# Moving the down products of three feed-forwards two blocks behind the up products, with every block turned by VectorE

## What is computed

```python
h2 = rms_norm(x, g_mlp[i])                                    # first block, D_FF = 4096
x = x + jnp.square(jax.nn.relu(h2 @ w_ff1[i])) @ w_ff2[i]

def swiglu(x, w_gate, w_up, w_down):                          # second block, twice, D_FF_2 = 2816
    return (jax.nn.silu(x @ w_gate) * (x @ w_up)) @ w_down    # added to x with FFN_RES = 0.5
```

## Time and profile before

| what | us |
|---|---|
| median of 3 runs | 977.59 |
| the profiled execution | 977.64 |
| its span, first to last instruction | 975.8 |
| TensorE busy | 968.6 |
| VectorE busy | 710.5 |
| ScalarE busy | 500.8 |
| mean granted clock of TensorE | 0.998 |

### The profile page before, as it was taken

The page is one execution under the profiler, slowest core; times in us unless marked ns, Lnnn a source line. Parts: engine busy times, 40 slices in busy tenths (PEclk is TensorE's granted clock), DMA queues, the critical chain, the costliest instruction groups (busy, mean ns, idle before and its releaser), DMA issues.

```text
span 975.8 us, 13212 instructions
## 1 busy us (share of the span) xinstructions
PE 968.6 (99%) x4800; PEld 809.0 (83%) x4800; DVE 710.5 (73%) x1187; ACT 500.8 (51%) x673; POOL 65.8 (7%) x97
## 2 busy tenths in 40 slices
PE   9999999999999999999999999999999999999997
PEld 7989888888888888888888888888887788888886
DVE  6746555478758888784778878786748877878784
ACT  7445555744465444444674444445648664444442
POOL 4101000011020000000120000000203020000000
PEclk9999999999999999999999999999999999999999
DMA  9755544444565555554565555644644255656531
GB/s 342 262 174 173 173 161 152 148 161 173 173 211 193 196 189 198 190 198 144 177 235 192 191 197 187 199 151 135 221 173 152 87 171 176 211 176 207 180 129 44
DMA packets 98726, 175.70 MB, mean 180 GB/s; under 512 B 5920, under 2 KB 54128, under 8 KB 98672
## 3 DMA queue, kind: packets, MB, share of 16 engines
q1 hardware_dynamic: 97024, 171.53, 52.2%
q0 software_dynamic: 1344, 3.19, 1.2%
q10 hardware_dynamic: 304, 0.27, 0.1%
HBM read 173.91 MB, written 1.05 MB: 179 GB/s over the span
## 4 chain that ended last, share of the span: by engine, by line
PE 99%; issue 0%; DVE 0%; ACT 0%; POOL 0%; POOLq 0%; ACTq 0%
PE bank L527 83%; PE bank L648 6%; PE bank L541 3%; PE bank L586 1%; PE bank L585 1%; PE bank L853 1%; PE bank L597 1%; PE bank L992 1%; PE bank L682 0%; PE bank L858 0%; PE bank L1054 0%; PE bank L598 0%; PE bank L599 0%; PE bank L617 0%; PE bank L993 0%
## 5 line engine op out<-in xcount | busy, mean ns | idle before, releaser
L527 PE MATMUL bank<-w_hi,hA 128*128 128x512 f32 (+1 forms) x1560 | 487.0, 390 | 0.0
L1585 DVE TENSOR_TENSOR w_lo<-raw,w_hi 128x2048 fp32r<-128x2048 f32 (+1 forms) x159 | 358.7, 2263 | 121.4 <-ACT w_hi L1129 120.6
L1129 ACT ACTIVATE w_hi<-raw 128x2048 fp32r<-128x2048 f32 (+1 forms) x162 | 306.2, 1894 | 186.1 <-PE bank L527 160.0
L527 PEld LDWEIGHTS bank<-w_hi,hA 128*128 128x128 f32 x1560 | 291.4, 188 | 59.2 <-issue 0.8
L527 PE MATMUL bank<-w_lo,hA 128*128 128x512 f32 (+1 forms) x780 | 297.0, 387 | 0.0
L527 PEld LDWEIGHTS bank<-w_lo,hA 128*128 128x128 f32 x780 | 146.6, 188 | 29.2
L1952 DVE STREAM_TRANSPOSE act_T<-act_f 32x128 f32<-32x128 f32 x288 | 87.1, 302 | 3.7
L527 PE MATMUL bank<-w_hi,fT_hi 128*128 128x512 f32 x232 | 71.7, 390 | 0.0
L527 PE MATMUL bank<-w_hi,fT_lo 128*128 128x512 f32 x232 | 71.5, 389 | 0.0
L527 PE MATMUL bank<-w_lo,fT_hi 128*128 128x512 f32 x232 | 71.5, 389 | 0.0
L648 PE MATMUL bank<-hA,w_hi 128*128 128x256 f32 x320 | 58.2, 284 | 0.0
(11 more groups left out here) (308 smaller groups left out, 970.1 us busy)
## 6 DMA issues: line engine op xcount, KB each, us to landing
raw<-in_w_in SPq DMA_DIRECT2D x74, 512.0 KB, 4.5
raw<-in_w_ff SPq DMA_DIRECT2D x64, 512.0 KB, 4.1
raw<-in_ffn_w_gate SPq DMA_DIRECT2D x44, 512.0 KB, 3.8
raw<-in_ffn_w_up SPq DMA_DIRECT2D x44, 512.0 KB, 4.7
raw<-in_ffn_w_down SPq DMA_DIRECT2D x44, 512.0 KB, 4.0
raw<-in_w_out SPq DMA_DIRECT2D x16, 512.0 KB, 4.3
raw<-in_w_branch_diff SPq DMA_DIRECT2D x8, 512.0 KB, 4.3
raw<-in_w_branch_ret SPq DMA_DIRECT2D x8, 512.0 KB, 4.3
```

Of the source, the lines that this page charges most:

```text
L527: mm = pe.matmul(o, a, w, start=first and t == 0 and m < len(outs), stop=last and t == n - 1 and m >= len(todo) - len(outs))
L1129: act.activation(w_hi[u % HI_SLOTS][:, 0:w], raw[u % RAW_SLOTS][:, 0:w], ACT.Copy).then_inc(hi_ready, 1)
L1585: vec.tensor_tensor(w_lo[u % RAW_SLOTS][:, 0:w], raw[u % RAW_SLOTS][:, 0:w], w_hi[u % HI_SLOTS][:, 0:w].bitcast(f32), ALU.subtract).then_i ...
```

## The change

The down products of all three feed-forwards follow two blocks behind the up products, in the queues of SyncE, TensorE, ScalarE and VectorE. TensorE runs up(0), up(1), up(2), down(0), up(3), down(1) and so on. After the last up product come three down products (in "ff" the products of the embedding stay ahead of the last one). Unit numbers follow that order. All blocks are computed with the tokens on the partitions and turned by VectorE. `ff_turn` is called no more, and `relu_wide`, `wide_low`, `wide_square` and `tall_split` are gone. `ff_up` now waits at block 1, too, for the products of block 0.

```diff
# SyncE: order of the loads
-        for j in range(2):
-            narrow(u + j, w_ff1, 4 * j, 4, 0, HALF)
+        for i in range(2):
+            for j in range(2):
+                narrow(u + 2 * i + j, w_ff1, 4 * j, 4, i * HALF, HALF)
...
-        for j in range(2):
-            wide(u + 30 + j, w_ff2, DFF - HALF + 2 * j * P)
+        for j in range(4):
+            wide(u + 28 + j, w_ff2, DFF - 2 * HALF + 2 * j * P)
...
# TensorE
-        def ff_up(u, name, i, steps, cols, du=0, di=0):
+        def ff_up(u, steps, du=0, di=0):
             for j in range(2):
                 for tb in range(TB):
-                    if j == 0 and i > 1:
+                    if j == 0:
                         pe.wait_ge(up_out, 2 * steps - 1 + tb + 2 * di)
...
-                if j == 0 and i == 1:
-                    ff_turn(name, i - 1, 2 * steps, cols, di)
...
         for i in range(1, last + 1):
-            relu_up(i) if i < last else relu_wide(i)
-            for j in range(2):
-                for tb in range(TB):
-                    mm = relu_down(i - 1, tb, j)
-                mm.then_inc(unit_used, 1)
+            relu_up(i)
+            for d in {1: (), last: (last - 2, last - 1)}.get(i, (i - 2,)):
+                for j in range(2):
+                    for tb in range(TB):
+                        mm = relu_down(d, tb, j)
+                    mm.then_inc(unit_used, 1)
...
-            step(1)
+            ff_up(u + 2, base + 1)
+            step(2)
             with pe.Fori(0, 2) as r:
-                for i in range(2, 6):
+                for i in range(3, 7):
                     step(i, r)
...
# ScalarE, first feed-forward
+        hi(U0["ff"] + 5)
+        relu_split(0)
+        hi(U0["ff"] + 6)
+        for tb in range(TB):
+            relu(1, tb)
...
# ScalarE, gated feed-forwards
             silu(0, 0)
             silu(0, 1)
             hi(u + 4)
+            hi(u + 5)
+            turned_split(0)
+            hi(u + 6)
+            silu(1, 0)
+            silu(1, 1)
...
+            hi(u + 33)
+            act.wait_ge(unit_used, u + 31)
+            turned_split(n - 1)
+            hi(u + 34)
...
# VectorE, first feed-forward
+        relu_turn(0)
+        lo(U0["ff"] + 5)
+        relu_low(0)
+        lo(U0["ff"] + 6)
+        for tb in range(TB):
+            square(1, tb)
+        relu_turn(1)
+
+        for i in range(2, DFF // HALF):
+            v = U0["ff"] + 4 * (i - 1)
             lo(v + 3)
...
+            relu_low(i - 1)
             lo(v + 4)
...
+            for tb in range(TB):
+                square(i, tb)
+            relu_turn(i)
+            lo(v + 5)
             lo(v + 6)
+        lo(U0["ff"] + 31)
+        relu_low(DFF // HALF - 1)
+        lo(U0["ff"] + 32)
...
# VectorE, gated feed-forwards
             multiply(0, 0)
             multiply(0, 1)
             lo(u + 4)
+            turn_act(0)
+            lo(u + 5)
+            turned_low(0)
+            lo(u + 6)
+            multiply(1, 0)
+            multiply(1, 1)
 
             def step(i, r=0):
-                v = u + 2 + 3 * (i - 1)
-                if i > 1:
-                    turn_act(i - 1, r)
+                v = u + 4 + 3 * (i - 2)
+                turn_act(i - 1, r)
+                if i > 2:
+                    lo(v + 2, 12 * r)
                 lo(v + 3, 12 * r)
-                if i == 1:
-                    for tb in range(TB):
-                        split((name, 0, tb))
-                else:
-                    turned_low(i - 1, r)
+                turned_low(i - 1, r)
                 lo(v + 4, 12 * r)
                 for tb in range(TB):
                     multiply(i, tb, r)
-                lo(v + 5, 12 * r)
...
+            turn_act(n - 1)
+            turned_low(n - 1)
+            lo(u + 33)
```

More of the change, by code:

```diff
@@ L837, in relu_up @@
                 mm.then_inc(unit_used, 1)
[L838 to L861, removed]
-                mm.then_inc(unit_used, 1)
         def relu_down(i, tb, j):
-            if i == 0:
-                turned(("ff", 0, tb))
-            else:
-                pe.wait_ge(f_ready, i + (i == DFF // HALF - 1 and j))
+            pe.wait_ge(f_ready, i + 1)
             if i == j == 0:
@@ L958, in gated @@
                             for m, (o, a, b) in enumerate(todo):
-                                mm = pe.matmul(o, a, b, start=c0 > HALF and (w, t, m) == (v + 2, 0, 0),
-                                               stop=(w, t, m) == (v + 3, 1, 2))
+                                mm = pe.matmul(o, a, b, start=c0 > HALF and (w, t, m) == (v, 0, 0),
+                                               stop=(w, t, m) == (v + 1, 1, 2))
                     mm.then_inc(last_half, 1)
@@ L1331, in _ @@
         split(("p",))
-        for i in range(1, DFF // HALF):
-            v = U0["ff"] + 2 + 4 * (i - 1)
+        hi(U0["ff"] + 5)
[5 more added lines that the diff above has]
+            v = U0["ff"] + 4 * (i - 1)
             hi(v + 3)
-            if i == 1:
-                for tb in range(TB):
-                    split(("ff", 0, tb))
+            relu_split(i - 1)
             hi(v + 4)
-            for b in range(2):
-                relu(i, b) if i < DFF // HALF - 1 else wide_low(i, b)
+            for tb in range(TB):
+                relu(i, tb)
             hi(v + 5)
-            if i < DFF // HALF - 1:
-                hi(v + 6)
-                relu_split(i)
-            else:
-                tall_split(i)
-                hi(v + 6)
+            hi(v + 6)
+        hi(U0["ff"] + 31)
+        relu_split(DFF // HALF - 1)
+        hi(U0["ff"] + 32)
         def ple_copy(tb):
@@ L1407, in gated @@
             hi(u + 4)
+            hi(u + 5)
[3 more added lines that the diff above has]
+            silu(1, 1)
             def step(i, r=0):
-                v = u + 2 + 3 * (i - 1)
+                v = u + 4 + 3 * (i - 2)
+                if i > 2:
+                    hi(v + 2, r)
                 hi(v + 3, r)
-                if i == 1:
-                    for tb in range(TB):
-                        split((name, 0, tb))
-                else:
-                    turned_split(i - 1, r)
+                turned_split(i - 1, r)
                 hi(v + 4, r)
@@ L1977, in step @@
                     multiply(i, tb, r)
-                lo(v + 5, 12 * r)
-            step(1)
+            step(2)
             with vec.Fori(0, 2) as r:
-                for i in range(2, 6):
+                for i in range(3, 7):
                     step(i, r)
-            v, i = u + 2 + 3 * (n - 2), n - 1
-            turn_act(i - 1)
-            turned_low(i - 1)
-            multiply(i, 0)
-            lo(v + 3)
-            split((name, i, 0))
-            lo(v + 4)
-            multiply(i, 1)
-            split((name, i, 1))
-            lo(v + 5)
+            turn_act(n - 1)
+            turned_low(n - 1)
+            lo(u + 33)
             if norm_out == "final":
```

144 lines of the change are left out of this document (42 added, 102 removed).

## The result

The changed kernel takes 998.21 us (median of 5 runs, 997.97 to 999.19), against 977.59 before. The ratio is 1.0213, with a 95% interval of 1.0202 to 1.0224, so it is 2.1% slower. The profiled execution took 997.97 us with a span of 995.8.

A forecast was written before the change was run, and what follows sets the result against it. The sum of TensorE's work was taken to bound the kernel until its last matmul, plus any new waits of TensorE: 977.64 - 2.9 (TensorE's savings) + 19.1 (waits) + 4.0 (clock) = 997.8 us, range 992.5 to 1002.

The forecast's parts named there:

- What TensorE saves: 24 transposes fewer in the three feed-forwards (2.6 us) and block 7 of "ff" in usual matmuls (0.3 us): 2.9 us less.
- The waits: TensorE waits for VectorE's queue at the start of each feed-forward: 6.0 us in "ff", 8.2 in "f1", 4.9 in "f2", together 19.1.
- Its second wait: In "f1" ahead of up(2): 4.0 us, turned into 2.0 by the slow matmuls behind the wait ahead of up(1).
- The clock: TensorE's clock falls in the waits; two falls, in "ff" and "f2", count in full at 2.0 us each: 4.0 us.
- The bounds of 1.6 to 2.8: Loss in us per fall of TensorE's clock, from a return of 3.2 to 5.6 us at half pace.
- The return in "f1": The clock's fall ahead of up(1) in "f1" is paid inside the wait for VectorE, so it adds nothing.
- No cost elsewhere: Loads, ends of the feed-forwards, lo(u+34) in "f1" and the tail behind the last matmul were to move at no cost.
- The turn of the last block: At the ends of "f1" and "f2": ready at 18.4 us, wanted by TensorE at 19.1; a late last turn had chance 0.05.
- No gain from two blocks behind: Down products two blocks behind give nothing back, because no wait of TensorE stood there before.
- the granted clock of the opening: Shown at full before the first matmuls; by it alone a return would be free and the sum 4.0 us lower.
- 390 ns for a transpose on TensorE: The skill's figure for a 128x128 transpose; by it the 24 would be 9.4 us and the forecast 6.8 us lower.

The follow-up runs named there:

- e9: e5 with silu(1) and multiply(1) of the gated feed-forwards moved ahead of the splits of block 0, hi(u+6) and lo(u+6); 976.59 us.
- e4: The changed kernel, but VectorE copies block 0 of each feed-forward in one instruction where it turned it in 16; 981.05 us.
- e2: The changed kernel without the wait of block 1 of the gated feed-forwards for the products of block 0; 1001.17 us.
- e3: The changed kernel with 76 matmuls that nobody reads put into TensorE's waits; 994.18 us.
- e12: The changed kernel with hi of the seventh unit moved ahead of the split of the turned block 0 on ScalarE, in all feed-forwards; 998.35 us.
- e1: The kernel before with one edit: block 1 of the gated feed-forwards waits for the products of block 0; 984.36 us.
- e6: The kernel before, down products one block behind, with only the turn of block 0 moved to VectorE; 991.82 us.
- e5: The changed kernel, but TensorE turns block 0 of each feed-forward inside up(1), and block 1 of the gated ones waits for nothing; 980.79 us.
- e8: The changed kernel with block 0 of "ff" turned by TensorE; gated block 1 uses a second buffer, is multiplied before block 0's turn and waits for nothing; 980.23 us.
- e11: e8 with lo of the next down product's unit moved ahead of the turn in every later block of the gated feed-forwards; 980.54 us.

## Why the prediction was right

The forecast was 997.8 us, the measured time 998.21. By its own steps:

- **What TensorE saves** (2.9 us). The instruction count is 4760, as forecast, and no transpose of act_f is left on TensorE. e9, which has 8 of the 24 transposes fewer, no wide block and no new wait, was to save 1.2 us and saved 1.1 against its rounds of before (0.3 to 2.1 by the interval). That agrees with the pricing of a transpose by its share of TensorE's path (0.109 us).
- **The waits** (19.1 us). The list was to have 17 to 19 us of them in all and has 15.3. "ff" 6.0 forecast, 5.9 measured. "f2" 0.4 and 4.5 forecast, 0.36 and 4.03 measured. "f1" 4.2 measured as 4.07. Its second wait is 0.93 us where I had 2.0, because the slow stretch between the two was longer than I took it (2.8 us lost, by the reading from 514.3 to 520.1, for 2.0). Idle and slow time in "f1" add to 7.8, against 8.2 that VectorE's queue was to dictate. e4 shows that these waits come from the turn of block 0, and e2 that the two of "f1" share one end.
- **The clock** (4.0 us). e3 measures 4.03. The parts differ from what I took: 2.5 in "ff" and 1.6 in "f2" for 2.0 each, and e12 has 1.3 and 2.7 there. So that two times 2.0 came out is in part luck: nothing in the prediction could tell a short return from a long one. The bounds of 1.6 to 2.8 took a return at exactly half the pace; it is 0.427 us for 0.227. The return in "f1" is absorbed, as forecast, and e1 and e2 show what it costs where it is not.
- **No cost elsewhere.** The turn of the last block, forecast with 0.7 us to spare, the products of the embedding and the loads show no wait of TensorE. In e4, which keeps all of them, no wait above 0.3 us is left beside those at block 1.
- **No gain from two blocks behind.** Forecast as nothing. e6 shows that with block 0 on VectorE it costs 7.6 us or more, and e9 that it is free once multiply(1) stands ahead of lo(u+6). Where it stays behind lo(u+6), e5 shows 2.5 us of wait even with the turn on TensorE. The prediction did not see this part, because the turn hid it: it would have been the next thing to be late.

The sum of the profile: 977.64 - 2.9, plus 15.3 us idle, plus 2.5 + 2.8 + 1.6 at the half clock, is 996.9, and 1.0 is left of the profiled 997.97. The restarts are a likely home for it: the last matmul before a wait counts as busy for 0.39 us, where in a row it takes 0.227, and there are five. e8 points the same way: with three waits of 3.3 us in all and the clock at 1.00 throughout, its profiled execution (980.15) is 1.2 us above 977.64 - 2.0 + 3.3. The prediction had no term for the restarts. Counted as it counted, the waits are 5.9 + 7.8 + 4.4 = 18.1 us for 19.1, and the missing 1.0 of restarts made up for that. The mechanism was right in each place; that the sum came within 0.4 us is partly luck.

The prediction set the granted clock of the opening, shown at full, against the slow matmuls there. The trace holds no entry of the clock before 6.28 us, and the view prints 1.00 where it has none. Behind the waits there is an entry, and it agrees with the pace: 0.50 where matmuls start 0.427 us apart.

The prediction weighed a figure of the Trainium skill, 390 ns for a transpose on TensorE ("VectorE: DVE Perf Modes", "The three transpose paths"). As a price of TensorE's path the runs don't bear it out: by it e9 would have saved 3.4 us where it saved 1.1. The page states the figure for bf16, and the blocks here are float32. The same page's advice ("Rules for kernel authors") to turn 128x128 blocks on TensorE was right for block 0 here, for another reason than the price: it keeps a turn of 5.05 to 7.18 us out of VectorE's queue.

## What to carry to other kernels

An engine with a quarter of its time to spare still delays the one that bounds, wherever a long operation enters its queue ahead of something short that frees a buffer: follow both queues by hand from the start of a stage, and ask what had covered that place before. Before you take work off that engine, try its order: put the operation that frees the other engine's buffer ahead of the work that is due a product later (e9). And price a wait of TensorE at its length plus the slow matmuls behind it, unless another wait follows that absorbs them (e2) or the wait is so short that the clock stays up (e8, e11: 1.5 and 1.6 us).

## What was not expected of the hardware

- The clock comes down for waits shorter than I had allowed. After the last matmul of the kernel before it took 2.1 us. Here the shortest that brought it down was 2.28 us (e6, "f2"), and the longest that left it up 2.02 us (e12, "f1"), each seen in one profiled execution. In e5, with 2.5 us of wait, the recorded clock was still 1.00 when the wait ended and read 0.63 in the next 2 us: the fall can come after the matmuls have started again.
- The price of a fall varies, and the length of the wait does not settle it. In the changed kernel it is 1.6 to 2.8 us each, from 3.4 to 5.8 us at the lower level, for waits of 4.0 to 5.9 us. In e12 the waits of 5.95 and 4.03 us have the two prices exchanged. What settles it no run here shows. A wait of TensorE of 2.5 us cost 2.8 + 1.6 us in e5.
